# VectorE's dense work one or two steps later in its order, row buffers 10 and 8 instead of 8 and 10, x loaded among the output weights

## The reference, cut to what matters

```python
q = jnp.einsum("td,de->te", tb, wq).reshape(-1, PEER_HEADS, 2, PEER_HALF)
sc = jnp.einsum("thjd,hjnd->thjn", q, subkeys)
s1, i1 = lax.top_k(sc[:, :, 0], PEER_TOPK); s2, i2 = lax.top_k(sc[:, :, 1], PEER_TOPK)
...
best, sel = lax.top_k(cand, PEER_TOPK)
idx = jnp.take_along_axis(cidx, sel, axis=-1)
g = jax.nn.softmax(best, axis=-1)
ue = jnp.take(u, idx, axis=0); ve = jnp.take(v, idx, axis=0)
a = jax.nn.gelu(jnp.einsum("thkd,td->thk", ue, tb), approximate=False)
return jnp.einsum("thk,thkd->td", g * a, ve)
```

## Time and profile before

| | us |
|---|---|
| median of 3 runs | 4090.52 |
| lowest, highest | 4090.32, 4098.42 |
| the profiled execution | 4068.56 |
| its span | 4066.8 |
| TensorE busy | 3190.2 (78%) |
| VectorE busy | 2504.1 (62%) |
| GpSimd busy | 2173.8 (53%) |
| ScalarE busy | 911.2 (22%) |
| moved by DMA | 1306.97 MB, 321 GB/s |

### The profile page before, as it was taken

One profiled execution on the slowest core, in us unless ns is written; L12 is line 12 of the kernel. 1 busy time (PEld: TensorE's weight loads), 2 busy tenths in 40 slices (PEclk: granted clock), 3 DMA queues, 4 the chain that ended last, 5 costly groups with the idle time before them and its releaser, 6 DMA issues.

```text
span 4066.8 us, 41006 instructions
## 1 busy us (share of the span) xinstructions
PE 3190.2 (78%) x13101; PEld 1795.1 (44%) x13101; DVE 2504.1 (62%) x6368; ACT 911.2 (22%) x1917; POOL 2173.8 (53%) x1892
## 2 busy tenths in 40 slices
PE   8989987866789865687677789874655799988994
PEld 5667564543445432345344455432333433463331
DVE  2133356577866557664887876556788944696542
ACT  1235211244421111112443431110111200121000
POOL 1000034556556457655665666547788766576664
PEclk9999998977789977899777779987855799868996
DMA  6443387999899899989899999989999999989998
GB/s 219 123 145 97 138 285 262 360 329 333 320 341 364 304 367 367 352 305 373 304 331 317 341 336 401 327 298 349 400 361 350 324 401 419 402 286 360 419 420 324
DMA packets 520902, 1306.97 MB, mean 321 GB/s; under 512 B 47120, under 2 KB 243280, under 8 KB 520688
## 3 DMA queue, kind: packets, MB, share of 16 engines
q0 software_dynamic: 267264, 973.20, 63.6%
q1 hardware_dynamic: 213024, 289.45, 20.6%
q10 hardware_dynamic: 40400, 41.70, 3.2%
HBM read 1252.15 MB, written 52.02 MB: 321 GB/s over the span
## 4 chain that ended last, share of the span: by engine, by line
PE 41%; DVE 20%; DMA 17%; POOL 8%; issue 5%; DVEq 5%; ACT 3%; SPq 1%; ACTq 0%; POOLq 0%
DMA G_v_rows<-in_peer_v,G_idxT 9%; PE scores L899 8%; DVE G_u_rows L2135 6%; PE scores L1783 6%; PE y_sum L2307 5%; POOL G_u_rows L775 5%; PE scores L2404 4%; PE scores L1787 4%; POOL G_v_rows L775 3%; DMA T_chunks<-in_peer_v 3%; PE scores L1872 3%; PE scores L1565 3%; PE scores L1977 2%; PE scores L1472 2%; PE o L1507 1%
## 5 line engine op out<-in xcount | busy, mean ns | idle before, releaser
L775 POOL DMA_INDIRECT G_u_rows<-in_peer_u,G_idx x1056 | 1254.3, 1188 | 1079.6 <-DVE G_dots L2135 687.9
L2135 DVE CUSTOM_DVE_ANT_0 G_u_rows<-G_u_rows,G_h 128x1024 f32<-128x1024 f32 x1056 | 1270.2, 1220 | 368.4 <-DMA G_u_rows<-in_peer_u,G_idx 344.0
L775 POOL DMA_INDIRECT G_v_rows<-in_peer_v,G_idxT x800 | 904.8, 1131 | 394.9 <-issue 229.0
L2307 PE MATMUL y_sum<-G_v_rows,G_zw 128*32 128x512 f32 x3200 | 521.9, 783 | 285.1 <-DMA G_v_rows<-in_peer_v,G_idxT 285.1
L2404 PE MATMUL scores<-T_chunks,T_spread_w 128*128 128x512 f32 x1024 | 466.9, 610 | 23.8 <-DMA T_chunks<-in_peer_v 21.1
L2307 PEld LDWEIGHTS y_sum<-G_v_rows,G_zw 128*32 128x32 f32 x3200 | 104.2, 131 | 566.4 <-issue 561.0
L2404 PEld LDWEIGHTS scores<-T_chunks,T_spread_w 128*128 128x128 f32 x1024 | 193.0, 194 | 299.9 <-issue 247.1
L899 PE MATMUL scores<-A_w_in,A_hT 128*128 128x256 f32 (+2 forms) x864 | 224.1, 420 | 24.7 <-DMA A_w_in<-in_w_in 17.3
L732 POOL MEMSET G_zw<- 128x1024 f32 x2 | 1.9, 964 | 395.9 <-SPq L694 395.9
L899 PEld LDWEIGHTS scores<-A_w_in,A_hT 128*128 128x128 f32 x864 | 170.5, 200 | 77.0 <-DMA A_w_in<-in_w_in 18.9
L1490 PE MATMUL turn<-ident,C_probs 128*128 128x128 f32 x635 | 135.8, 332 | 60.6 <-ACT C_pT L1598 51.2
(11 more groups left out here) (317 smaller groups left out, 4629.3 us busy)
## 6 DMA issues: line engine op xcount, KB each, us to landing
T_chunks<-in_peer_v SPq DMA_DIRECT2D x64, 1024.0 KB, 9.0
A_w_in<-in_w_in SPq DMA_DIRECT2D x24, 1024.0 KB, 12.4
D_w_gate<-in_w_gate SPq DMA_DIRECT2D x24, 1024.0 KB, 9.2
G_u_rows<-in_peer_u,G_idx POOLq DMA_INDIRECT x1056, 7.6
G_v_rows<-in_peer_v,G_idxT POOLq DMA_INDIRECT x800, 7.5
DF_w<-in_w_gate SPq DMA_DIRECT2D x12, 1024.0 KB, 12.9
DF_w<-in_peer_wq SPq DMA_DIRECT2D x12, 1024.0 KB, 9.7
F_w_q<-in_peer_wq SPq DMA_DIRECT2D x12, 1024.0 KB, 7.0
```

What stands on the lines that cost most here:

```text
L775: pool.indirect_dma_start(out=buf[:, :], out_offset=None, in_=table, in_offset=bass.IndirectOffsetOnAxis(ap=rows, axis=0)).then_inc(signal ...
L2135: dve.tensor_tensor_reduce(out=self.u_rows[slot][:, :], in0=self.u_rows[slot][:, :], in1=self.h2[t % 2][:, :], scale=1.0, scalar=0.0, op0= ...
L2307: last = pe.matmul(self.ps_y[32 * c:32 * (c + 1), cols], self.zw[b % 2][:, lo:lo + 32], self.v_rows[self.ring_v.slot[4 * quad + c]][:, col ...
```

## The change

Three edits. `SLOTS_U, SLOTS_V` go from 8, 10 to 10, 8; the sum of the buffers stays 18. VectorE's plan, and only VectorE's, puts each dense tick of spans 1 and 2 one step later (the score stage two, where the due times allow it). Counted over the 601 ticks: 368 ticks of inputs, attend, merge and out of spans 1 and 2 move by one, 16 score ticks by two, 3 by one, 13 score ticks of spans 1 and 2 and all of span 0 by none. And `out_sp` issues x of tile 0 between the output weight rows, and x of tile 1 after the gain, both ahead of the first score weights.

```diff
-SLOTS_U, SLOTS_V = 8, 10
+SLOTS_U, SLOTS_V = 10, 8
...
+DVE_BEHIND = {"inputs": 1, "memory": 0, "attend": 1, "merge": 1, "out": 1, "score": 2}
...
-    def plan(self):
+    def plan(self, late=False):
...
+        shift = DVE_BEHIND if late else dict.fromkeys(DVE_BEHIND, 0)
...
             for name, cost in own:
                 sofar += cost
+                behind = shift[name] if sp.i else 0
                 if name != "score":
-                    out.append(done + int((turn - done) * sofar / dense))
+                    out.append(max(out[-1:] + [done + int((turn - done) * sofar / dense) + behind]))
                     continue
...
-                out.append(max(0, min(steps, ready)))
-            done = out[-1]
+                out.append(max(out[-1], min(steps + behind, ready)))
+                end = max(0, min(steps, ready))
+            done = end
...
-    def weave(self, dense, steps):
+    def weave(self, dense, steps, late=False):
...
-        plan, tick, done = self.plan(), 0, 0
+        plan, tick, done = self.plan(late), 0, 0
...
-        self.load_w_o(eng, m, range(len(self.D[i]["w_o"]), DC))
+        head = len(self.D[i]["w_o"])
+        middle = (head + DC) // 2
+
+        def load(t):
+            if t >= 2:
+                eng.wait_ge(self.e_out[t % 2], self.e_out0[t % 2][i] + 32 * (t // 2))
+            r = sp.rows[t]
+            eng.dma_start(m["x1"][t % 2][0:r, :], a["x_all"][sp.tiles[t] * P:sp.tiles[t] * P + r, :]).then_inc(self.e_x[t % 2], 16)
+
+        self.load_w_o(eng, m, range(head, middle))
+        load(0)
+        self.load_w_o(eng, m, range(middle, DC))
         eng.dma_start(m["g_ffn"][:, :], a["norm_ffn"].to_broadcast([P, D])).then_inc(self.e_g, 16)
+        if nt > 1:
+            load(1)
         self.load_score(eng, sp, 0)
...
         for t in range(nt):
             if t >= 2:
-                eng.wait_ge(self.e_out[t % 2], self.e_out0[t % 2][i] + 32 * (t // 2))
-            r = sp.rows[t]
-            eng.dma_start(m["x1"][t % 2][0:r, :], a["x_all"][sp.tiles[t] * P:sp.tiles[t] * P + r, :]).then_inc(self.e_x[t % 2], 16)
+                load(t)
             if t:
                 store(t - 1)
             yield
...
-            k.weave(k.dense(k.inputs_dve, k.memory_dve, k.attend_dve, k.merge_dve, k.out_dve, k.score_dve, dve), k.experts_dve(dve))
+            k.weave(k.dense(k.inputs_dve, k.memory_dve, k.attend_dve, k.merge_dve, k.out_dve, k.score_dve, dve), k.experts_dve(dve), late=True)
```

## The result

| | before | changed |
|---|---|---|
| median, us | 4090.52 (4078.35 to 4098.42, 7 runs) | 4109.62 (4101.66 to 4117.25, 7 runs) |
| ratio | | 1.0047, 95% interval 1.003 to 1.0063 |
| profiled execution, us | 4068.56 | 4110.52 |
| its span | 4066.8 | 4108.8 |
| TensorE, VectorE, GpSimd busy | 3190.2, 2504.1, 2173.8 | 3226.9, 2502.5, 2168.0 |

Slower by 0.5%, 19 us; the two profiled executions differ by 42 us, since the first one was 22 us under its median. In a second set of twelve runs the changed kernel stood at 1.0037 (1.0023 to 1.0051).

The account below looks back on a forecast made before the run. No single engine bounds it; the bound changes by stage. Terms 9 + 3 + 8 - 16 + 13 + 4 + 0 = +21 us on 4090.5 gave about 4112; range 4048 to 4158, the forecast's own 4099 to 4135.

Parts of the forecast that it names:

- The end: Last ten quads of the kernel: with eight v buffers 6.9 us each in place of 5.5, +13 us.
- Streaming: While streaming, with eight v buffers: landings may shrink from 19.8 to 16 us; +4 us, bounds 0 and 80.
- Rival B: Streaming: the landing does not shrink, or only by half; +40 to +80 us, 4150 to 4190; chance 0.10.
- The u ring in score: Score stages: ten u buffers let GpSimd gather further before stopping; 8 us gained each, -16 for both.
- Rival D: Score stages: GpSimd's added gathers only lengthen the landings, ring term 0; +37 us, 4128; chance 0.05.
- Rival A: Score stages: GpSimd's whole 75 us of waiting won; -38 us, 4052, with attend waits down to 4025; chance 0.33.
- The stage ends and inputs: VectorE leaves stages one step later, +9 us together; its norms in inputs come one dot later, +3 us.
- inputs +3: Inputs: TensorE and ScalarE wait for a few VectorE norms, one dot later each; +3 us (0 to 8).
- The gelu chain in attend: Attend stages: VectorE's `weigh` at c = 1 waits for a gelu, up to 2.5 us; +8 us, bounds 0 and 42.
- No gain inside attend: Attend stages: the shift leaves the chain's pace unchanged, 0; any gain bounded by exp waits, down to -30 us.
- x: Out stages: VectorE's 21.85 us wait shrinks by 3 at most, the projection is late next; 0 us (-8 to +3).
- The mark of 17: Out: a sign of being right, the wait for x down to about 17 us with out no shorter.

## Why the prediction was right, step by step

4112 was forecast and 4109.6 measured. The stages that do not repeat (attend 2 and score 2, attend 1 to a lesser degree) make any single pair of traces a bad judge, so the terms are read from the fourteen profiles, grouped by the edits that touch a stage (the ring of six is left out where its ring touches it). Stage lengths are from the first TensorE instruction of one stage to that of the next; the end is from the last block of streamed table to the last quad. Means in us, with the number of profiles:

| stage | without the edit | with it | difference | forecast |
|---|---|---|---|---|
| inputs 1 + 2 (shift) | 206.2 + 229.3 (9) | 219.3 + 223.9 (5) | +7.7 | +3 |
| merge 1 + 2 (shift) | 442.6 (9) | 438.3 (5) | -4.3 | 0 |
| out 1 + 2 (shift) | 123.1 (6) | 130.7 (5) | +7.6 | +4.8, of the ends |
| attend 1 (shift, rings 8/10) | 338.7 (8) | 351.6 (3) | +13 | +4 (half of 8) |
| attend 1 (shift, rings 10/8) | | 343.2 (3) | +4.5 | +4 |
| score 1 + 2 (shift and u ring 10) | 526.3 (4) | 511.2 (3) | -15 | -12 (ring -16, end of score 1 +4.1) |
| streaming (v ring 8) | 745.6 (8) | 751.7 (5) | +6 | +4 |
| end (v ring 8) | 82.3 (8) | 95.3 (5) | +13 | +13 |

The differences that are there for rings 10 and 8 sum to 19.5 us; attend 2 and building stand aside. Attend 1 and the score stages differ among profiles without the edit by 8 and 14 us, so single rows of theirs are rough.

- **The end.** +13, the term: 6.8 to 6.9 us a quad in five profiles. The rule that set it, which gather after a weighing completes the next quad but one, also gave the ring of six within 1 us a quad.
- **Streaming.** Rival B (the v ring decides) falls. The time from a v gather's issue to its last landing record, the median over the streaming part, is 18.8 to 20.8 us with ten v buffers (eight profiles), 14.2 to 15.1 with eight (five) and 8.3 with six, while a quad's pace is 14.2, 14.3 and 14.6 us. The landing was queueing, as argued; it fell a little further than the 15 to 17 us forecast. Even at six, where the same sum with a landing of 14 us would give 20 us a quad, the pace gave way by 3% only.
- **The u ring in score.** -16 forecast. With the u ring at ten the two stages are 511 us without the shift and 511 with it, with the u ring at eight 526 and 522 (four profiles with score's shift). So the gain looks like the ring's: 15 us without the shift, from one profile, and about 10 us with it. The longest of the three profiles with both edits (517.9) and the shortest of those with neither (517.6) meet, so the size is known to some 5 us at best. The two-step shift is worth 0 to 5 us, where I had its end at a loss of 4.1. Rival D (the added gathers only lengthen the landings) falls by the shorter stages, which run at 383 and 364 GB/s (364 and 354 before). The Trainium skill (DMA: Bandwidth & Descriptors, Specifications) has about 358 GB/s for a core, as half of what a stack gives its two cores. Both stages pass it, and so does the 413 of streaming; here one core runs alone, and as a limit on it the figure does not hold. Rival A (the whole stop of GpSimd is won) falls too. GpSimd's stops in the two score stages together were 78 us before and are 62 in the changed kernel, 16 less, as forecast; one long stop is left in each, 25.6 us for VectorE's dots in score 1 and 25.8 for `y_sum` in score 2, where the v ring took over.
- **The stage ends and inputs.** Inputs, merge and out together are +11, forecast +7.8, near by two errors. TensorE's waits at the start of the out stages did not grow by 1 us, as I had written, but shrank, to 7.58 and 9.33 from 8.17 and 11.39; the loss sits inside out, the gain in merge. Most of the loss in out has a row: TensorE's last wait there, for VectorE's norm of the third tile, is 8.1 and 8.0 us in all five profiles with the shift in out, and 5.3 and 5.0 in the others (but for the second with six v buffers). Before, out 1:

```profile
1438.33 1.11 PE L1887 MATMUL turn<-ident,E_h 128*128 128x128 f32 x4 [5.31 <-DVE E_h L1926]
```

  The changed kernel:

```profile
1454.33 1.11 PE L1902 MATMUL turn<-ident,E_h 128*128 128x128 f32 x4 [8.13 <-DVE E_h L1941]
```

  And "inputs +3" was too small. Inputs 1 of the changed kernel, its waits (total, times, longest), then rows of TensorE and VectorE:

```profile
DVE G_einv L2111 <- ACT G_egate L2241: 14.7, 1, 14.7
...
PE turn L891 <- DVEq L1115: 12.8, 3, 5.8
...
672.91 0.17 DVE L2126 TENSOR_TENSOR G_weights<-G_gelus,G_gates 128x16 f32<-128x16 f32 x1 [2.44 <-ACT G_gelus L2276]
...
745.88 0.90 PE L891 MATMUL turn<-ident,A_cq 128*128 128x128 f32 x3 [5.75 <-DVEq L1115]
```

  In the first profile of before the second was 5.4 us and the first was not there. The second is where the time goes: TensorE falls behind three unshifted profiles at the norms of two tiles, by about 7 and 5 us, and by little elsewhere. I had one plain dot of 1.22 us for each norm. But the step put ahead of the one carries `weigh` with its wait of 2.44 us for a gelu (4.1 us from the dot's start to the norm), and the step put ahead of the other a ranking piece of 2.5 us (3.6 us). The first wait, 14.7 us long, is of the same kind as `weigh`'s: VectorE's reciprocal of the gates' sum waits for a ScalarE result that stands in ScalarE's order behind dense work. But it costs nothing: it stands at the end of inputs 1, where VectorE now waits 14.73 and then 13.16 us for attend's first scores. Before, it was one wait:

```profile
826.26 0.56 DVE L1661 TENSOR_REDUCE C_ntop<-scores 128x1 f32<-128x384 f32 x1 [26.12 <-PE scores L1472]
```

  Inputs 2, 5 us shorter, gives part of the loss back: TensorE's wait for its norms is 4.6 us there, where it was 9.2 in the first profile of before.
- **The gelu chain in attend.** It exists, as forecast: in the changed kernel `weigh` waits 5.1 us in attend 1, where it had not waited, and in attend 2 12.1 us in four waits that end with the gelu, where it was 1.7. The second profile of the changed kernel has 5.1 and 11.3. That is nearly twice the +8, and the longest wait, 6.6 us, is beyond the 2.5 that I had as the most. What the stages pay for it is not shown: attend 1 is 4.5 us longer with the rings of the changed kernel, which is hardly more than it moves by itself, and attend 2 cannot be told. With the old rings the shift in attend alone cost 24 us. So the kind was right and the size was not confirmed. "No gain inside attend" held.
- **x.** 0 forecast, 0.9991 (0.9974 to 1.0009) measured. What remains of the wait is the projection, named as late next: 19.9 us in out 1 and 17.0 in out 2. The mark of 17 did not follow from the working, which let 21.85 us shrink by 3 at most.
- **A mark that failed.** I had written that GpSimd's waits for dots would shrink by less than those for `y_sum` grow. They shrank by 524 and grew by 486 us; as a sign of the loss this says nothing: the sum of both fell by 38 us while the kernel became 19 us slower.
- **What my working lacked.** I priced the v ring outside the end and streaming at nothing, and the three edits as if they added. By the medians neither holds. By ratios the parts are +0.0061, +0.0047 and -0.0009, 0.0099 together, and the whole is 0.0042 (mean of its two measurements): 0.0057 less, 23 us, with an uncertainty of some 0.0034. Rings alone were +25 where my terms give +1 to +5. The profiles show part of it in attend 1, 13 against 4.5 us for the shift, and point to attend 2: without the shift it is 487 us with ten v buffers (five profiles, 478 to 504) and 505 with eight or six (three, 503.5 to 506.2); with the shift it is 498 with ten (three) and 490 with eight (three, 483 to 498). But the two profiles with eight v buffers and no shift also have 43.6 and 48.5 us of late TensorE results in that stage, and the kernel before, with 45.6, took 504.1. So in attend 2 the cost of the shorter ring and the gain from having both are not shown by the profiles; that the ring makes such late results more frequent is one reading, chance the other. What the medians do show is enough for the verdict: the forecast's total came out right partly by luck, since it left out a cost of about 20 us of the rings and a gain of about the same size from having shift and rings together. Why the v ring costs anything outside the end and streaming is open. In attend 2 with eight v buffers the last row of each quad had landed over 3 us before TensorE weighed it, so TensorE did not wait for rows, and VectorE's dots waited 6 us in all, as before. GpSimd's stops for `y_sum` in attend 2 of the rings alone (106 us, none before) took the place of those for dots (127 before, 12 there).

## What to carry to other kernels

Size a ring by asking which gather after a release completes the next unit of work: (weighing) + (issues up to that gather) + (landing) gave the pace at ten and eight buffers, and within 1 us of 10.4 at six, and the landing to put in is the one at the shortened ring, not the one measured while the DMA engines were full. Before a trace's stage difference is given to an edit, profile the same kernel twice; here one stage of 480 us moved by 26 us on its own, more than the whole change was worth, while merge, out, streaming and the end repeated within 3 us. Look in both for waits on "remote" too: their sum told the long profiles of that stage from the short ones. When one engine's order is shifted against the others, list every value that it reads from another engine within a step or two of the shift, in all stages, and ask of each step put ahead of a value what it carries. A new wait in the trace is not yet a cost: look whether the same engine stood idle at that place before.

## What the runs showed of the hardware that I had not expected

- The same kernel's attend 2 took 477.9 and 504.1 us in two profiled executions at nearly the same busy times. In the three groups of runs that kernel's times reach from 4074 to 4122 us, and one chip's median was 0.4% above the others'.
- In thirteen of fourteen profiles some of TensorE's matmuls raise their semaphore late, 2.5 to 4.5 us at the median and up to 13.3 us after the end that the trace gives them; the waits for them sum to 27 to 142 us a profile.
- The landing time of a 512 KB gather in full DMA engines fell with the number of v buffers: about 20, 14.6 and 8.3 us with ten, eight and six, at 419, 413 and 408 GB/s in a like stretch. I had expected a floor near the 15 to 17 us of the forecast.
- Moving two buffers from one ring to the other moved most of GpSimd's stops, 688 and 166 us before, 164 and 652 after; their sum went from 854 to 816 us.
